# Gate and up products of an FFN as seven block products each, with the first weight sums on GpSimd

## What is computed

```python
D_FF = ((8 * D_MODEL // 3 + 127) // 128) * 128      # 2816, D_MODEL = 1024
def swiglu(x, w_gu, w_down):
    gu = x @ w_gu
    return (jax.nn.silu(gu[..., :D_FF]) * gu[..., D_FF:]) @ w_down
...
        x = x + 0.5 * swiglu(rms_norm(x, p['ffn1_norm'][l]), p['ffn1_w_gu'][l], p['ffn1_w_down'][l])
```

## Time and profile before

| | |
|---|---|
| runs | 2139.01, 2137.51, 2139.36 us; median 2139.01 |
| profiled execution, span | 2136.6 us |
| TensorE, VectorE, ScalarE, GpSimd busy | 98%, 45%, 33%, 3% |
| TensorE clock granted, mean | 0.990 of full |
| HBM traffic | 171.43 MB by DMA, 80 GB/s mean |

### The profile page before, as it was taken

The page is one execution under the profiler, slowest core; times in us unless marked ns, Lnnn a source line. Parts: engine busy times, 40 slices in busy tenths (PEclk is TensorE's granted clock), DMA queues, the critical chain, the costliest instruction groups (busy, mean ns, idle before and its releaser), DMA issues.

```text
span 2136.6 us, 36911 instructions
## 1 busy us (share of the span) xinstructions
PE 2097.5 (98%) x15589; PEld 2075.3 (97%) x15589; DVE 961.9 (45%) x1290; ACT 704.7 (33%) x929; POOL 65.7 (3%) x87
## 2 busy tenths in 40 slices
PE   7999999999999999999999999999999999999996
PEld 6999999999999999999999999999978999999996
DVE  5442344478754432444544323444483544333434
ACT  4221333236743321222433212223273433212222
POOL 1000000011200000000000000000010000000001
PEclk9999999999999999999999999999998999999998
DMA  4222223222222222222132312222200222312221
GB/s 167 80 93 84 69 80 100 76 70 80 82 80 89 82 95 69 79 89 98 60 111 82 101 63 85 83 96 70 71 11 1 85 83 88 99 59 89 86 81 44
DMA packets 45992, 171.43 MB, mean 80 GB/s; under 512 B 5313, under 2 KB 7777, under 8 KB 45905
## 3 DMA queue, kind: packets, MB, share of 16 engines
q1 hardware_dynamic: 44128, 166.09, 23.5%
q0 software_dynamic: 784, 3.04, 0.4%
q10 hardware_dynamic: 1008, 1.31, 0.2%
HBM read 167.72 MB, written 3.69 MB: 80 GB/s over the span
## 4 chain that ended last, share of the span: by engine, by line
PE 94%; DVE 3%; ACT 1%; issue 1%; DMA 1%; SPq 0%; DVEq 0%; ACTq 0%
PE ps L422 89%; PE ps L593 1%; PE ps L618 1%; PE ps L603 1%; DMA x<-xT 1%; PE ps L700 1%; PE ps L714 0%; PE ps L713 0%; DVE arena L1153 0%; DVE rstd L1049 0%; DVE xs_lo L1037 0%; DVE x L1414 0%; DVE w_lo L1026 0%; PE ps L462 0%; ACT w_hi L745 0%
## 5 line engine op out<-in xcount | busy, mean ns | idle before, releaser
L745 ACT ACTIVATE w_hi<-raw 128x1024 fp32r<-128x1024 f32 (+1 forms) x285 | 323.0, 1133 | 1222.0 <-PE ps L422 1215.5
L422 PE MATMUL ps<-xs_hi,w_hi 128*128 128x288 f32 (+2 forms) x3232 | 696.3, 297 | 15.1 <-DVE xs_lo L1037 12.2
L422 PE MATMUL ps<-xs_hi,w_lo 128*128 128x288 f32 (+2 forms) x3232 | 693.7, 296 | 0.0
L422 PE MATMUL ps<-xs_lo,w_hi 128*128 128x288 f32 (+2 forms) x3232 | 693.6, 296 | 0.0
L422 PEld LDWEIGHTS ps<-xs_hi,w_hi 128*128 128x128 f32 x3232 | 524.3, 189 | 18.2 <-issue 14.0
L422 PEld LDWEIGHTS ps<-xs_hi,w_lo 128*128 128x128 f32 x3232 | 524.3, 189 | 0.0
L422 PEld LDWEIGHTS ps<-xs_lo,w_hi 128*128 128x128 f32 x3232 | 524.3, 189 | 0.0
L1026 DVE TENSOR_TENSOR w_lo<-raw,w_hi 128x1024 fp32r<-128x1024 f32 (+1 forms) x285 | 376.3, 1320 | 85.6 <-ACT w_hi L745 85.0
L422 PE MATMUL ps<-act_hi,w_hi 128*128 128x288 f32 (+1 forms) x1696 | 363.0, 296 | 3.4 <-ACT arena L865 3.1
L422 PE MATMUL ps<-act_lo,w_hi 128*128 128x288 f32 (+1 forms) x1696 | 362.7, 295 | 0.0
L422 PE MATMUL ps<-act_hi,w_lo 128*128 128x288 f32 (+1 forms) x1696 | 362.6, 295 | 0.0
(11 more groups left out here) (164 smaller groups left out, 889.5 us busy)
## 6 DMA issues: line engine op xcount, KB each, us to landing
raw<-w_gu SPq DMA_DIRECT2D x175, 512.0 KB, 3.3
raw<-w_dn SPq DMA_DIRECT2D x64, 704.0 KB, 4.1
raw<-w_rec SPq DMA_DIRECT2D x20, 512.0 KB, 3.2
raw<-w_out SPq DMA_DIRECT2D x8, 512.0 KB, 3.3
raw<-w_q SPq DMA_DIRECT2D x8, 512.0 KB, 3.3
raw<-w_o SPq DMA_DIRECT2D x8, 512.0 KB, 3.3
x<-xT ACTq DMA_DIRECT2D x4, 288.0 KB, 8.6
x<-xT SPq DMA_DIRECT2D x4, 288.0 KB, 12.1
```

Of the source, the lines that this page charges most:

```text
L422: ins = nc.tensor.matmul(ps[:, 2 * slot + c, 0:width], wv(a, w, kw), halves(b, o, width), start=first and n == 0, stop=last and n == 2)
L745: nc.scalar.activation(w_hi[:, par, 0:kt * P], raw[:, slot, 0:kt * P], ACT.Copy).then_inc(hi_made, 1)
```

## The change

Each pair of a gate and an up tile is seen as a 2x2 block matrix: rows are gate and up, columns the first and second four k-tiles (A11, A12 of gate; A21, A22 of up). The operand x is 2x2 as well: first and second four k-tiles by first and second 288 tokens. The product of the two is made by seven block products of Strassen's kind in place of eight, in Winograd's form. Each block product is 4 k-tiles x 3 passes = 12 matmuls of 288 columns into one bank (`product`, L556). TensorE's order in a *window* (one pair, g) is P1, then P4 of the pair before, P2, P5, P6, P3, P7. Three banks hold a pair; P6, P7 and P4 go on adding into the bank of P1, P3 into that of P5, so ScalarE copies a bank's state in between (s1, s5, s2, s7) and VectorE adds what belongs together.

The weight blocks need four sums. X1 = A21 + A22 and X4 = A21 + A11 are one GpSimd instruction of 1024 elements (`sum_x14`, L1750; the first operand is broadcast, and X4 is written over it). X2 and X3 are two VectorE instructions of 512 (L1291, L1294). The hi parts and residues of A11, A12, A22, X1 to X4 are seven blocks of 512, in four instructions on ScalarE and four on VectorE. The hi and lo parts of all seven have one buffer each; the raw weights have two buffers of a pair.

x is split once per FFN into seven blocks for each of the four pairs of k-tiles (`x_sums`, `x_lo`), behind scaled copies by ScalarE. rstd multiplies only the gate; that of up is moved behind the down product, whose eviction is two instructions now. An FFN has three chunks of 8, 8 and 6 pairs, each followed by 8 down jobs. The FFN code is unrolled. The first norm's squares are summed by 16 matmuls instead of 2; GpSimd's and VectorE's part in them is gone, and so is the early start on a quarter of the first weight tile. A new pair's weights (two loads of 512 KB) wait for the residues of the pair two before, or, at the start of a chunk, for the last residue made from those buffers.

GpSimd's queue in order: the sums of FFN 0, the recurrence's work, the sums of FFN 1, the keys' copies, the sums of FFN 2, attention's biases, the sums of FFN 3.

The diff, cut to its core:

```diff
...
+            def pair(g, g0, c0):
+                if g - g0 >= 2:
+                    sp.wait_ge(a22_lo_made, g - 1)
+                    sp.wait_ge(x43_lo_made, g - 1)
+                elif c0 > 0:
+                    a, b = run_of[c0 - 1]
+                    last = max(j for j in range(a, b) if slot_of[j] // 2 == g % 2)
+                    sp.wait_ge(lo_made, last + 1)
+                load_pair(g)
...
+            def product(bank, w, b, start, tiles=range(N_PAIR), stop=True):
+                for i, p in enumerate(tiles):
+                    for n, (wt, xt) in enumerate(((g_hi, xs_hi), (g_hi, xs_lo), (g_lo, xs_hi))):
+                        ins = nc.tensor.matmul(ps[:, bank, 0:HT], gv(wt, w)[:, 0, p * P:(p + 1) * P],
+                                               xb(xt, p, b)[:, 0, :], start=start and i == n == 0,
+                                               stop=stop and i == len(tiles) - 1 and n == 2,
+                                               skip_group_check=True)
+                return ins
+            def p4(g):
+                pe.wait_ge(a22_lo_made, g + 1)
+                pe.wait_ge(snapv2_made, g + 1)
+                product(bank_a(g), A22, T4, False).then_inc(p4_done, 1)
+            def p637(g):
+                a = bank_a(g)
+                pe.wait_ge(snap1_made, g + 1)
+                product(a, X2, T2, False, stop=False).then_inc(p6_done, 1)
+                pe.wait_ge(x43_lo_made, g + 1)
+                pe.wait_ge(snap5_made, g + 1)
+                product(a + 2, X3, B22, False).then_inc(p3_done, 1)
+                pe.wait_ge(snapv1_made, g + 1)
+                product(a, X4, T3, False, stop=False).then_inc(p7_done, 1)
...
+            def pair(g, g0, c0, middle=None):
+                a = bank_a(g)
+                pe.wait_ge(a_lo_made, g + 1)
+                if g - g0 >= 2:
+                    pe.wait_ge(hid_made, g - 1)
+                elif g == g0:
+                    pe.wait_ge(dve_evac, evac(c0 - 2))
+                product(a, A11, B11, True, stop=False).then_inc(p1_done, 1)
+                if g > g0:
+                    p4(g - 1)
+                product(a + 1, A12, B21, True).then_inc(p2_done, 1)
+                if middle is not None:
+                    middle()
+                if g == g0:
+                    pe.wait_ge(dve_evac, evac(c0 - 1))
+                pe.wait_ge(x12_lo_made, g + 1)
+                product(a + 2, X1, T1, True, stop=False).then_inc(p5_done, 1)
+                p637(g)
...
-                    ins = nc.tensor.matmul(ps[:, 4 + c, 0:width], ones[:, :], ssum[:, o:o + width],
-                                           start=True, stop=True)
+                    for m in range(KD):
+                        pe.wait_ge(first_sq_made, m + 1)
+                        for c, (o, width) in enumerate(EVEN):
+                            ins = nc.tensor.matmul(ps[:, 6 + c, 0:width], ones[:, :], first_sq[:, m, o:o + width],
+                                                   start=m == 0, stop=m == KD - 1)
                 ins.then_inc(stat_sum, 1)
...
+            def window(g, g0, g1, c0, stat):
+                if g > g0:
+                    snap_v2(g - 1)
+                hi_x43(g)
+                act.wait_ge(p1_done, g + 1)
+                if g:
+                    act.wait_ge(y_sum_made, g)
+                nc.scalar.activation(s1, ps[:, bank_a(g), 0:HT], ACT.Copy).then_inc(snap1_made, 1)
+                if stat is not None:
+                    root(stat)
+                if g > g0:
+                    silu(g - 1)
+                hi_a22(g)
+                if g + 1 < g1:
+                    hi_a(g + 1)
+                else:
+                    prep(c0)
+                if g > g0:
+                    hid_hi(g - 1, g - 1 - g0, c0)
+                act.wait_ge(p5_done, g + 1)
+                if g:
+                    act.wait_ge(c22_made, g)
+                nc.scalar.activation(s5, ps[:, bank_a(g) + 2, 0:HT], ACT.Copy).then_inc(snap5_made, 1)
+                act.wait_ge(p6_done, g + 1)
+                nc.scalar.activation(s2, ps[:, bank_a(g), 0:HT], ACT.Copy).then_inc(snapv1_made, 1)
+                if g + 1 < g1:
+                    hi_x12(g + 1)
+                else:
+                    prep(c0 + 1)
...
+            def key_value():
+                j, f, g = base["kv"], 2, FT * 2
+                hi_a(g)
+                act.wait_ge(job_done, j)
+                for i, p in enumerate(PORDER[f]):
+                    for b in range(2):
+                        x_scaled_to(f, p, X_TEMPS[f][i], b)
+                root(3)
+                x_hi_first(f, 0)
+                x_hi_rest(f, 0)
+                hi_x12(g)
+                for i, used in ((1, 4), (2, 7), (3, None)):
...
+            def sum_x23(g):
+                dve.wait_ge(x14_made, g + 1)
+                dve.wait_ge(a_lo_made, g + 1)
+                nc.vector.tensor_tensor(pair_raw(g, R_A11), pair_raw(g, R_X1), pair_raw(g, R_A11),
+                                        ALU.add).then_inc(x2_made, 1)
+                dve.wait_ge(x2_made, g + 1)
+                nc.vector.tensor_tensor(pair_raw(g, R_A12), pair_raw(g, R_A11), pair_raw(g, R_A12),
+                                        ALU.add).then_inc(x3_made, 1)
+            def gate_out_of(g):
+                dve.wait_ge(p2_done, g + 1)
+                dve.wait_ge(p3_done, g + 1)
+                dve.wait_ge(snap1_made, g + 1)
+                dve.wait_ge(snapv1_made, g + 1)
+                if g:
+                    dve.wait_ge(hid_ready, g)
+                b = bank_a(g) + 1
+                nc.vector.tensor_tensor(two(y), ps[:, b:b + 2, 0:HT], two(s12), ALU.add).then_inc(y_sum_made, 1)
+                dve.wait_ge(y_sum_made, g + 1)
+                nc.vector.tensor_tensor(y, y, rstd[:, :], ALU.mult).then_inc(y_scaled, 1)
...
+            def up_second(g):
+                dve.wait_ge(snapv2_made, g + 1)
+                dve.wait_ge(snap5_made, g + 1)
+                nc.vector.tensor_tensor(c22, s7, s5, ALU.add).then_inc(c22_made, 1)
+            def hidden(g):
+                dve.wait_ge(silu_made, g + 1)
+                dve.wait_ge(c22_made, g + 1)
+                nc.vector.tensor_tensor(y[:, HT:NT], y[:, HT:NT], c22, ALU.mult)
+                dve.wait_ge(p4_done, g + 1)
+                nc.vector.tensor_tensor(y[:, 0:HT], ps[:, bank_a(g), 0:HT], y[:, 0:HT], ALU.mult).then_inc(hid_made, 1)
+            def hid_lo(g, tile):
+                dve.wait_ge(hid_hi_made, g + 1)
+                sub(act_tile(act_lo, tile), y, act_tile(act_hi, tile).bitcast(F32), hid_ready)
+            def window(g, g0, g1, c0):
+                if g > g0:
+                    gate_out_of(g - 1)
+                lo_x43(g)
+                if g > g0:
+                    up_second(g - 1)
+                    hidden(g - 1)
+                lo_a22(g)
+                if g + 1 < g1:
+                    lo_a(g + 1)
+                else:
+                    prep(c0)
+                if g > g0:
+                    hid_lo(g - 1, g - 1 - g0)
+                if g + 1 < g1:
+                    sum_x23(g + 1)
+                    lo_x12(g + 1)
+                else:
+                    prep(c0 + 1)
...
+                        dve.wait_ge(job_done, j + 1)
+                        own(nc.vector.scalar_tensor_tensor(acc, acc, -0.5, two(rstd[:, :]), ALU.mult, ALU.mult))
+                        if j:
+                            dve.wait_ge(dve_evac, evac(j - 1))
+                        nc.vector.tensor_tensor(two(x[:, n, :]), acc, two(x[:, n, :]), ALU.add).then_inc(dve_evac, 1)
+                        prep_next(j)
...
+            def x_sums(f, i):
+                t = X_TEMPS[f][i]
+                dve.wait_ge(xg_made, 2 * (N_PAIR * f + i + 1))
+                own(nc.vector.tensor_tensor(t[:, T1:T3 + 1, :], t[:, B11:B22 + 1:2, :],
+                                            t[:, B12:B12 + 1, :].broadcast_to([P, 2, HT]), ALU.subtract))
+                own(nc.vector.scalar_tensor_tensor(t[:, T2, :], t[:, B22, :], -1.0, t[:, T1, :],
+                                                   ALU.mult, ALU.subtract))
+                nc.vector.scalar_tensor_tensor(t[:, T4, :], t[:, T2, :], -1.0, t[:, B21, :],
+                                               ALU.mult, ALU.subtract).then_inc(cmb_sums, 1)
...
-                    def unit(j, u, up_evac, par, slot, tile_at, prep_a, prep_b):
-                        dve.wait_ge(job_done, j + 1)
-                        nc.vector.tensor_tensor(two(gate_t[:, par, :]), ps2(slot), two(rstd[:, :]),
-                                                ALU.mult).then_inc(dve_evac, 1)
-                        prep_a()
-                        dve.wait_ge(job_done, j + 2)
-                        nc.vector.tensor_tensor(two(up_t[:, par, :]), ps2(1 - slot), two(rstd[:, :]),
-                                                ALU.mult).then_inc(dve_evac, 1)
```

(12 more changed lines are left out.)

837 lines of the change are left out of this document (502 added, 335 removed).

## The result

The changed kernel takes 2060.76 us (median of 4 runs, 2056.85 to 2061.54) against 2139.19 us for the kernel before, a ratio of 0.963 (95% interval 0.962 to 0.965): 78 us faster, where 2061 was forecast. The sum came out right to a microsecond, its terms did not: the loop cost almost nothing, the starts of FFN 0, 1 and 3 more than was allowed. The profiled execution has a span of 2058.7 us, 77.9 us less than before.

The account below looks back on a forecast made before the run. TensorE, busy 98% of the span, was taken as the bound: matmul count times pitch. 2136.6 - 140.8 + 10 + 14 + 18 + 18 + 3 = 2058.8, plus 2.4 from span to median: 2061 us, range 2028 to 2105.

Parts of the forecast that it names:

- the loop: Steady windows: VectorE's work plus its loss to GpSimd's sum takes 11.3 to 11.4 us, a little over TensorE's 11.2.
- What is removed: Block products on TensorE: 84 matmuls instead of 96 for each of 88 pairs, at 0.1333 us: 140.8 us less.
- GpSimd's sum: X1 and X4 in each window: 1024 elements on GpSimd take 2.41 us, beside VectorE's own 9.3 us.
- What VectorE loses by it: In each window VectorE loses 2.03 us of the 2.41 us GpSimd sum.
- The term of 10 us: P3 late by 0.1 to 0.3 us a window, taken as 0.13 over 76 windows: +10 us (0 to 46).
- rival 1: GpSimd's sum costs nothing in the windows, falling where VectorE reads PSUM or waits: 2051 us; chance 0.2.
- Rival 2: Shared port excludes fully and the sum takes 2.8 us: every window 11.8 us, +46 instead of +10, 2097 us; chance 0.2.
- Rival 3: Slower than before: the VectorE and GpSimd loop outgrows the saving, from a GpSimd sum of about 3.4 us; chance 0.08.
- The starts of FFN 1 and 3: Behind an out product: last tile pair's stall, root and reciprocal delay TensorE about 7 us each: +14 us (8 to 20).
- FFN 2: Start behind keys and values: queue order makes TensorE stand about 10 us, first pair ends late: +18 us (10 to 24).
- FFN 0: Kernel start: weights land about 13 us, VectorE's splits and 16 matmuls on squares delay TensorE: +18 us (10 to 25).
- Small terms: Two-instruction down eviction, +0.8 us at the end, and possible late residues beside down jobs: +3 us (0 to 8).

Follow-up runs that it names:

- the extra columns: Changed kernel with GpSimd adding 256 or 512 more columns ahead of its sum in each of 88 pairs: 2072.95 and 2102.04 us.
- the reordered run: Changed kernel with root and reciprocal first in their queues ahead of FFN 2, first split before key eviction, value eviction before later tile pairs: 2059.60 us.
- the run with the late root: Changed kernel with the root and its table load behind the copy of P5's bank in the first window of FFN 0, 1 and 3: 2051.52 us.

## Why the prediction was right, and where it was not

**What is removed** was exact: steady chunks run at 0.1333 us a matmul, twelve in one bank in a row change nothing, and no window has gaps inside a product.

**GpSimd's sum** was sized well, 2.40 us free where 2.41 was worked out. What VectorE has to do without it was right: 9.3 us a window with a wait of 0.5, and 8.9 busy by the run without the sum. **What VectorE loses by it** was the wrong step: 2.03 us forecast, 1.38 in the mean by the runs with and without it. Part of the sum falls on the gate sum, which reads PSUM and is not held. One window at 230 us shows it (VectorE, then GpSimd):

```profile
230.32 0.75 DVE L1306 TENSOR_TENSOR temp<-ps,temp 128x576 f32<-128x576 f32 x1
231.11 2.18 DVE L1308 TENSOR_TENSOR temp<-temp,rstd 128x576 f32<-128x576 f32 x1
```

```profile
230.27 2.41 POOL L1750 TENSOR_TENSOR raw<-raw 128x1024 f32<-128x1024 f32 x1 [8.27 <-DMA raw<-w_gu]
```

Of 2.41 us only 1.42 are lost, in the scaling alone (2.18 against 0.76). I read the earlier trace rows as "a part of the sum is always free" and should have asked which instructions stood beside it. And the sum was placed behind X4/X3's residue, 2.6 us into the window; the weights landed when they were ready for the gate sum, a window position that moved with the loads (this sum starts at 230.27 us and the next at 241.02, 10.75 us apart where a window is 11.2). With 0.65 us less the loop lies under TensorE's 11.2. **The term of 10 us measured 1.1**, all of it in the second chunk of FFN 0. That is rival 1's windows, though not for its reason alone: the sum does hold VectorE, and the extra columns show that the room left beside it is 0.8 to 1.0 us.

**Rival 2**, the shared port in full. The Trainium skill, "SBUF — State Buffer", section "SBUF: two separate sides", says that a VectorE instruction with two SBUF inputs and a GpSimd one that reads SBUF exclude each other for the whole instruction. The runs agree to the letter: held for the whole rest of the sum with two SBUF operands, not at all with one in PSUM. What was wrong in the rival was to charge the full sum to every window. **Rival 3** needed a sum of 3.4 us; the form with a broadcast operand, written over its own source, takes the 2.4 us that had been worked out from plain sums.

**The starts of FFN 1 and 3**, 7 us each, measured 10.0 and 10.5 (11.3 less 0.8 at the end). Of the 10.0 some 1.4 lie in the recurrence, which took 127.8 us before and 129.2 after, by the clock behind a stop that both kernels have. The parts that were named are there: the first P3 waits 1.09 us (1.4 forecast), the second 1.97 (2.4 to 4), and in FFN 1 the last tile pair's residues hold up TensorE for 1.1 (about 2). In the second is a term that nobody named: behind the reciprocal ScalarE loads its table for silu, 1.28 us, ahead of the copy of P5's bank. Left out was GpSimd's second sum, which stretches A's residue to 3.41 us just ahead of the last addition to x: TensorE waits 2.65 and 2.67 us for it, and 0.48 and 0.79 in the run without the sum. The lower clock stands behind two of FFN 3's stops, about 1.6 us each, and behind none of FFN 1's. The last 1.6 to 1.8 us of each stay open.

**FFN 2**: 18 forecast, 18.1 measured, with a gap of 10.4 us where "about 10" stood, and the first pair's last product late by VectorE's pace. The reason given was half right. The gap was where the queues put it, but the reordered run shows that it isn't what costs the 18 us: VectorE's 32 us of work set them in both orders.

**FFN 0**, 18 forecast, 22.4 measured (23.5 less the window's 1.1). The first weights landed at 13.0 us, as forecast. The last x residue ended at 35.26 us instead of 33.5; GpSimd's second sum, at 20.18 us, holds VectorE for 2 us on that path. The squares took 8.1 us (6.6 forecast from the earlier trace rows); the second window began at 50.8 instead of 46, and ended near 65.8 instead of 59.3, 1.6 us of that at the low clock. That is 6.5 us late where 4.4 are missing, since the kernel before lost more than the earlier trace rows shows: behind 33.49 us its next 12 matmuls took 3.04 us at a granted clock of 0.50, instead of 1.6.

**Small terms**: 3 forecast; 0.8 us at the end as worked out, and no residue late beside the down jobs. The sentence that TensorE hardly waited before left out another 9 us of waits, in FFN 0, the recurrence, attention and at the end; some 6 us of them are there after the change too.

So 10 + 14 + 18 + 18 + 3 = 63 stands against 1.1 + 20.5 + 18.1 + 22.4 + 0.8 = 62.9. The total fits by luck. The starts were put 11 us too low (50 forecast, 61.0 measured), the windows and the small terms 11 us too high (13 against 1.9). The price of GpSimd's sum was put at 10 us and into the windows; by the run without it, with the early load and the clock taken off, it is some 6 us, nearly all of it at the starts.

## What to carry to other kernels

Work given to GpSimd is not taken off VectorE where both read two SBUF operands: price it at the time for which VectorE is held, place it beside VectorE's PSUM-reading instructions, and count it apart for steady loops (where there is room) and for starts (where VectorE is last). At a start, ask of each instruction that is moved what stands behind it in every in-order queue, the other engines' too: one such move cost 4 us, another took 5.5 us of waits away. Where an engine is busy through the whole start, moving the gaps about gained nothing. And look into a run for everything that differs: an instruction added at the very start went with a load that landed 4.5 us earlier, which looked like the price of the sum.

## What the runs showed of the hardware

- A free GpSimd sum of 1024 fp32 elements takes 2.40 us, VectorE's 1.22 us. Beside it a VectorE instruction with two SBUF operands waits to its end, one with a PSUM operand runs at 0.75 to 0.76 us.
- A stop of TensorE can cost more than its length, and not each time: behind 1.97 us at 61 us the granted clock was 0.58 for 4.1 us (12 matmuls, 1.6 us), behind 1.97 us at 646 us of the same execution it was 1.00. Of 25 such stops of 1.96 to 1.99 us 15 had the lower clock behind them, of 53 of 0.81 to 1.54 us at the same matmul none.
- A table load on ScalarE took 1.28 us, and the next activation started right behind it (56.52 to 57.81 us).
- Executions differ in stages that no edit touches: attention took 161.3 us in the changed kernel's profiled execution and 158.5 to 161.3 in the others. At least 1.6 us of it is the clock: behind a stop of 1.25 us it was 0.75 over 4.5 us in the changed kernel and 1.00 in the run with the late root. Differences of 3 us between two profiled spans were therefore read by stages, not as a whole.
